# Gates of the attention branch ahead of its products, with the last delta-rule chain between their quarters

## What is computed

```python
proj = h @ w_in + b_in
aq, ak, av, dq, dk_, dv_, dz, db, da, ga, gb = split_cols(proj, IN_SPLITS)
o_att = sliding_window_sink_attention(rope(aq), rope(ak), av, att_sinks)
qkv = silu(causal_depthwise_conv(concat(dq, dk_, dv_), dn_conv_w))
o_dn = gated_rms_norm(gated_delta_rule_chunked(q, k, v, g, beta), dz, dn_norm_g)
y_att = o_att @ w_br_att
y_dn = o_dn @ w_br_dn
merged = sigmoid(ga) * y_att + sigmoid(gb) * y_dn
mix = merged @ w_out
h = layer_norm(ALPHA * h + mix)      # then SwiGLU, a gated input embedding and a second norm
```

## Time and profile before

| | us |
|---|---|
| median of 3 runs | 2249.12 (2247.03 to 2253.12) |
| the profiled execution | 2246.78 |
| its span, first to last instruction | 2245.0 |
| TensorE busy | 2143.2 |
| VectorE busy | 1297.4 |
| ScalarE busy | 1051.5 |
| POOL busy | 70.5 |

### The profile page before, as it was taken

The page is one execution under the profiler, slowest core; times in us unless marked ns, Lnnn a source line. Parts: engine busy times, 40 slices in busy tenths (PEclk is TensorE's granted clock), DMA queues, the critical chain, the costliest instruction groups (busy, mean ns, idle before and its releaser), DMA issues.

```text
span 2245.0 us, 39722 instructions
## 1 busy us (share of the span) xinstructions
PE 2143.2 (95%) x14959; PEld 1986.5 (88%) x14959; DVE 1297.4 (58%) x2182; ACT 1051.5 (47%) x1907; POOL 70.5 (3%) x65
## 2 busy tenths in 40 slices
PE   7999989999899997899999998999999999999997
PEld 6889889889888896799999986899999999998885
DVE  3657665766667655454555557665555555555555
ACT  2446354553554544444544444544444444444442
POOL 1000110100101001000000000000000000000000
PEclk7999999999999999899999999999999999999998
DMA  6564222232232221355555574555555555566552
GB/s 221 187 194 141 90 94 93 76 111 80 88 104 83 93 93 56 103 180 184 177 181 186 172 284 143 188 195 180 179 185 178 187 187 183 176 225 200 189 191 90
DMA packets 279401, 345.13 MB, mean 154 GB/s; under 512 B 6272, under 2 KB 227536, under 8 KB 277936
## 3 DMA queue, kind: packets, MB, share of 16 engines
q1 hardware_dynamic: 277696, 334.78, 46.0%
q0 software_dynamic: 1648, 9.57, 1.1%
HBM read 342.04 MB, written 2.10 MB: 153 GB/s over the span
## 4 chain that ended last, share of the span: by engine, by line
PE 86%; DVE 5%; ACT 5%; issue 3%; DMA 1%; DVEq 0%; ACTq 0%; SPq 0%
PE dense L457 18%; PE dense L458 17%; PE dense L459 17%; PE dense L469 8%; PE dense L470 8%; PE dense L471 8%; PE chain L607 2%; PE chain L604 1%; ACT hi L868 1%; PE chain L595 1%; PE chain L643 1%; PE chain L673 1%; PE chain L626 1%; PE chain L614 1%; PE chain L642 1%
## 5 line engine op out<-in xcount | busy, mean ns | idle before, releaser
L1157 DVE TENSOR_TENSOR lo<-raw,hi 128x512 fp32r<-128x512 f32 x1256 | 846.3, 691 | 615.6 <-ACT hi L868 612.6
L868 ACT ACTIVATE hi<-raw 128x512 fp32r<-128x512 f32 x1256 | 764.7, 629 | 586.6 <-PE dense L459 316.6
L457 PE MATMUL dense<-xh,hi 128*128 128x256 f32 x2944 | 860.5, 292 | 0.0
L459 PE MATMUL dense<-xh,lo 128*128 128x256 f32 x2944 | 835.9, 284 | 0.0
L458 PE MATMUL dense<-xl,hi 128*128 128x256 f32 x2944 | 835.9, 284 | 0.0
L457 PEld LDWEIGHTS dense<-xh,hi 128*128 128x128 f32 x2944 | 567.1, 193 | 21.5 <-issue 13.4
L458 PEld LDWEIGHTS dense<-xl,hi 128*128 128x128 f32 x2944 | 567.7, 193 | 3.6 <-issue 3.6
L459 PEld LDWEIGHTS dense<-xh,lo 128*128 128x128 f32 x2944 | 567.3, 193 | 0.0
L469 PE MATMUL dense<-hi,xh 128*128 128x512 f32 x416 | 163.3, 393 | 4.6 <-issue 3.1
L470 PE MATMUL dense<-hi,xl 128*128 128x512 f32 x416 | 162.9, 391 | 0.0
L471 PE MATMUL dense<-lo,xh 128*128 128x512 f32 x416 | 162.8, 391 | 0.0
(11 more groups left out here) (283 smaller groups left out, 1926.0 us busy)
## 6 DMA issues: line engine op xcount, KB each, us to landing
raw<-in_w_in_dram SPq DMA_DIRECT2D x116, 1024.0 KB, 5.0
raw<-in_w_ffn_gate_dram SPq DMA_DIRECT2D x44, 1024.0 KB, 4.9
raw<-in_w_ffn_up_dram SPq DMA_DIRECT2D x44, 1024.0 KB, 4.9
raw<-in_w_ffn_down_dram SPq DMA_DIRECT2D x44, 1024.0 KB, 5.1
raw<-in_w_br_att_dram SPq DMA_DIRECT2D x16, 1024.0 KB, 5.1
raw<-in_w_br_dn_dram SPq DMA_DIRECT2D x16, 1024.0 KB, 5.3
raw<-in_w_out_dram SPq DMA_DIRECT2D x16, 1024.0 KB, 5.2
raw<-in_w_ple_gate_dram SPq DMA_DIRECT2D x16, 1024.0 KB, 5.1
```

Source lines behind the costliest of these rows:

```text
L457: pe.matmul(o, wh, mh[:, k, :], start=(k == 0), stop=False)
L459: mm = pe.matmul(o, wl, mh[:, k, :], start=False, stop=(k == KT - 1))
L868: act.activation(hi[:, pos.slot(n), :], raw[:, slot, off:off + 512], ACT.Copy).then_inc(sem("hi_ready"), 1)
L1157: dve.tensor_tensor(lo[:, pos.slot(n), :], raw[:, slot, off:off + 512], hi[:, pos.slot(n), :].bitcast(F32), ALU.subtract).then_inc(sem("lo ...
```

## The change

The attention branch no longer goes group by group. All 64 gate quarters come first, right behind the mixer loop, alternating between the two pairs of banks, and each group's tanh is written straight to its place in `merged`. Behind quarter `1 + (c + 1) * 56 // 31` stands stage c of the last chain: stage -1 behind quarter 1, then 0 to 29 behind 2, 4, 6, 8, 10, 11, 13 and so on to 55, 56 quarters for 31 stages. The splits of the attention output stand beside quarters 56 to 63. Then come the 64 quarters of o_att @ w_br_att, also alternating between banks, and one VectorE product per group turns `merged` from tanh to gated product in place. The delta branch is as before.

`merged` moves to a place of its own behind the chain's buffers; the buffers of keys and values for the attention (`kTall`, `vall`), done by then, move to share it. POOL loads `res` as soon as the attention output has been split, and the norm's parameters after the delta branch. SP issues the same units in the new order.

```diff
-TAIL = (0, 4, 6, 9, 12, 17, 20, 23)
+LAST_AT = {1 + (c + 1) * 56 // 31: c for c in range(-1, 30)}
@@ sync
-            for off, w, base in ((GA, A["w_br_att"][0], U_YA), (GB, A["w_br_dn"][0], U_YD)):
-                with sp.Fori(0, 8) as j:
+            for j in range(8):
+                for h in range(2):
+                    load(Pos(4 * U_GA), 2 * j + h, unit_cols(w_in, h, slice(GA + 256 * j, GA + 256 * j + 256)))
...
@@ gpsimd
-            pool.wait_ge(sem("m_lo"), 8)
+            pool.wait_ge(sem("b_lo"), 8)
             pool.dma_start(res[:], A["x"][0].rearrange("(t p) n -> p t n", p=P)).then_inc(sem("res_in"), 16)
+            pool.wait_ge(sem("quarter_done"), 4 * U_OUT)
@@ tensor
-            for k in range(NORMS - LAG, 30):
-                chain_stage(k, PAIRS - 1, False)
-                if k == 0:
+            for n in range(64):
+                j = n // 8
+                if n == 0:
                     pe.wait_ge(sem("pad2"), PAIRS)
-                if k in TAIL:
-                    cols_quarter(Pos(4 * U_YA), TAIL.index(k), TAIL.index(k), 2, xh, xl)
...
+                elif n == 8:
+                    pe.wait_ge(sem("z_in"), PAIRS)
+                elif n % 8 == 0:
+                    pe.wait_ge(sem("gate"), j - 1)
+                cols_quarter(Pos(4 * U_GA), n, n % 8, 2 * ((j + 1) % 2), xh, xl)
+                if n in LAST_AT:
+                    chain_stage(LAST_AT[n], PAIRS - 1, False)
+
+            for n in range(16):
+                if n % 8 == 0:
+                    pe.wait_ge(sem("gate"), 7 + n // 8)
+                if n < 8:
+                    pe.wait_ge(sem("b_lo"), n + 1)
+                cols_quarter(Pos(4 * U_AT), n, n % 8, 2 * ((n // 8 + 1) % 2), bh, bl)
+            with pe.Fori(1, 4) as m:
+                for n in range(16):
+                    if n % 8 == 0:
+                        pe.wait_ge(sem("prod"), 2 * m - 1 + n // 8)
+                    cols_quarter(Pos(4 * U_AT, 16, m), n, n % 8, 2 * ((n // 8 + 1) % 2), bh, bl)
@@ scalar
+            def gate_out(j):
+
+                act.wait_ge(sem("quarter_done"), 4 * U_GA + 8 * j + 8)
+                for f in range(2):
+                    r = act.activation(merged[:, 2 * j + f, :], dense[:, 2 * ((j + 1) % 2) + f, 0:T], ACT.Tanh,
+                                       bias=hbias[:, 2 * j + f:2 * j + f + 1], scale=0.5)
+                r.then_inc(sem("gate"), 1)
+
+            for n in range(64):
+                split(Pos(4 * U_GA + LEAD), n)
+                if n in LAST_AT:
+                    c = LAST_AT[n]
+                    if c == -1:
+                        chain_k(0, PAIRS - 1)
+                        chain_k("norms", PAIRS - 1)
+                    elif c > 0:
+                        chain_k(c, PAIRS - 1)
+                        y_copy(c, PAIRS - 1)
+                if n >= 56:
+                    b = n - 56
+                    if b == 0:
+                        act.wait_ge(sem("on"), 8)
...
+                if n % 8 == 7:
+                    gate_out(n // 8)
@@ vector
+            dve.wait_ge(sem("gate"), 8)
+            with dve.Fori(0, 4) as m:
+                for n in range(16):
+                    split(Pos(4 * U_AT + LEAD, 16, m), n)
+                    if n % 8 == 7:
+                        e = n // 8
+                        dve.wait_ge(sem("quarter_done"), 4 * U_AT + 8 + 8 * e + 16 * m)
+                        g = merged[:, ds(4 * m + 2 * e, 2), :]
+                        b0 = 2 * ((e + 1) % 2)
+                        dve.scalar_tensor_tensor(g, g, 1.0, dense[:, b0:b0 + 2, 0:T], ALU.add,
+                                                 ALU.mult).then_inc(sem("prod"), 1)
```

More of the change, by code:

```diff
@@ L231, in build @@
         vn = place("vn", [P, 2, P])
+        at[0] += -at[0] % 512
+        mg_at = at[0]
+        kTall = place("kTall", [P, PAIRS, 192])
+        vall = place("vall", [P, PAIRS, 2, HD])
         o = [at[0]]
@@ L753, in _, with branch @@
                 mixer_turn(i, True)
-            for k in range(NORMS - LAG, 30):
-                chain_stage(k, PAIRS - 1, False)
-                if k == 0:
+            for n in range(64):
+                j = n // 8
+                if n == 0:
                     pe.wait_ge(sem("pad2"), PAIRS)
-                if k in TAIL:
-                    cols_quarter(Pos(4 * U_YA), TAIL.index(k), TAIL.index(k), 2, xh, xl)
[L762 to L772, removed]
+                elif n == 8:
[16 more added lines that the diff above has]
+                    cols_quarter(Pos(4 * U_AT, 16, m), n, n % 8, 2 * ((n // 8 + 1) % 2), bh, bl)
+            def branch(j, first):
+                pos = Pos(4 * U_YD, 16, j)
+                for k in range(16):
+                    if k == 0:
+                        pe.wait_ge(sem("prod"), 7) if first else pe.wait_ge(sem("gate"), j + 8)
+                    if k == 8:
+                        pe.wait_ge(sem("prod"), j + 8)
+                    if k >= 8:
+                        if first:
+                            pe.wait_ge(sem("b_lo"), 8 + k - 7)
                         cols_quarter(pos, k, k - 8, 0, bh, bl)
@@ L775, in branch @@
                         cols_quarter(pos, k, k, 2, xh, xl)
-            branch(Pos(4 * U_YA, 16, 0), 0, 0, (None, ("z_in", PAIRS)), start=8)
+            branch(0, True)
             with pe.Fori(1, 8) as j:
[L780 to L783, removed]
+                branch(j, False)
             pe.wait_ge(sem("gate"), 16)
@@ L1068, in gates @@
+            with act.Fori(0, 4) as m:
+                for n in range(16):
+                    split(Pos(4 * U_AT + LEAD, 16, m), n)
+            def gates(pos, j, gt_used):
                 for k in range(16):
-                    if k >= start:
-                        split(pos, k)
+                    split(pos, k)
                     if k == 8 - 1:
                         act.wait_ge(sem("quarter_done"), pos.val(8 - LEAD))
-                        if gt_used is not None:
-                            act.wait_ge(sem(gt_used[0]), gt_used[1])
+                        act.wait_ge(sem("prod"), gt_used)
@@ L1484, in _ @@
                 mixer_turn(i, True)
[L1485 to L1507, removed]
+            for n in range(64):
+                split(Pos(4 * U_GA + LEAD), n)
+                if n in LAST_AT:
+                    c = LAST_AT[n]
+                    if c == -1:
+                        chain_k(0, PAIRS - 1)
+                        chain_k("norms", PAIRS - 1)
+                    elif c > 0:
+                        chain_k(c, PAIRS - 1)
+                if n >= 56:
+                    b = n - 56
+                    dve.wait_ge(sem("b_hi"), b + 1)
+                    dve.tensor_tensor(bl[:, 2 * b:2 * b + 2, :].rearrange("p u (t c) -> p u t c", t=TT), att_cols(b),
+                                      bh[:, 2 * b:2 * b + 2, :].rearrange("p u (t c) -> p u t c", t=TT).bitcast(F32),
+                                      ALU.subtract).then_inc(sem("b_lo"), 1)
```

46 lines of the change are left out of this document (19 added, 27 removed).

## The result

The changed kernel took 2215.2 us (median of 4 runs, 2212.7 to 2216.5) beside 2248.1 us for the kernel before (4 runs, 2245.4 to 2253.1). The ratio is 0.985, with a 95% interval of 0.983 to 0.986: 32.8 us faster. Forecast were 2217.5 us, in a range of 2211 to 2228.

A forecast was written before the change was run, and what follows sets the result against it. TensorE's queue was taken to bound the kernel. The region from loop end to delta branch falls from 247.8 to 216.2 us, saving 31.6: 2246.8 - 31.6 = 2215.2 profiled, plus 2.3 gives 2217.5 us, range 2211 to 2228.

The forecast's parts named there:

- What binds: Whole kernel: TensorE, busy for 95% of the span, sets the end with its queue.
- The sum: End of mixer loop to first delta-branch quarter: 184.3 + 31.4 + 0.5 = 216.2 us, against 247.8 before.
- Chain: Last head pair's stages between quarters: 28.2 us priced from the mixer loop plus 3.2 for lengthened quarters, 31.4 us.
- Waits that stay: TensorE in the new tail: only POOL's first inverse level still makes it wait, 0.5 us.
- The key wait: Normed keys in the last chain: the loop's 1.9 us wait goes, with a slack of about 1 us.
- The seam: Between gate quarters and attention products: the 5.7 us wait for split attention rows is hidden by 11.5 us of gate work.
- The clock: New tail: full clock taken for the sum; granted clock 0.98 or more expected, 0.96 kept for the range.
- rival 2: New tail's clock doesn't come back: 4 to 5 us lost at 0.96, 15 at 0.87; chance 0.17 shared with waits.
- Parts costed at nothing: Gate tanh into merged, VectorE's wait and product, SP's order, POOL's earlier x load, ScalarE's tables: 0 us taken.
- The waits only thin out: New tail: late keys, late copies and small scan waits return 7 of 31.6 us, 2223; chance 0.17 shared with clock.
- The queue runs dry: New tail: chain stages hold back ScalarE's and VectorE's splits; slower from 1.2 us a stage; slower given 0.04.
- the signs asked for: Profile after: region about 216 us, no wait over 1 us, clock 0.98 or more, rest of kernel within 2 us.

The follow-up runs named there:

- the late load: Changed kernel with POOL's 2 MB load of x put back to where it was, behind the split of merged: 2214.9 us against 2215.2.
- the three that go on from the change: Changed kernel with attention query rotation moved earlier, 2190.5 us; that plus z's tanh and product behind normed keys and queries, 2196.2; or in the scan, 2191.1.
- the stages packed: Changed kernel with the last chain's 31 stages packed among the first 8 gate quarters, the other 56 following bare: 2242.7 us.
- one stage a quarter: Changed kernel with one stage of the last chain behind each of gate quarters 1 to 31: 2219.9 us.
- the z gate behind the norms: Changed kernel with query rotation moved earlier, plus the tanh of z and its product put behind the normed keys and queries: 2196.2 us.
- the early rotation alone: Changed kernel with the mixer loop's rotation of attention queries moved from quarter 5 to quarter 1: 2190.5 us.

## Why the prediction was right

- *What binds.* TensorE's queue sets the end and nothing behind the region moves: shown by the 1151.6 us behind it, the same in both profiles.
- *The sum.* Region after: forecast 216.2 us, measured 216.5. Dense quarters: 184.3, and 184.32 without the chain. Chain: 31.4 forecast, 32.2 measured with its wait, 31.8 without. Taking stages' prices from the loop's rows, first matmul to next dense matmul plus the lengthened quarter, was good to 0.4 us in sum. The lengthening went in as estimates (0.15 and 0.07 us a stage, 0.4 behind the norms), which no run measured singly, so errors in them may have cancelled.
- *Waits that stay.* The POOL wait of 0.4 us (0.5 forecast) and nothing else. The key wait is gone with 5 quarters and 1.5 us with 3.
- *The seam.* Its 5.7 us wait went, as forecast, but its share is less sharp than I had it: alone it gave 8.0 us in the medians and 2.6 in the region of the one profile.
- *The clock.* Full over the new tail, as the sum had it; the dip or two of rival 2 didn't come, in this profile or in the four others that have this tail (the late load and the three that go on from the change). The Trainium skill ("TensorE: Matmul & The Clock Gate", HAM oscillation) has repeated idle time between groups of matmuls bring the clock down. The new tail has 27 stages between groups of quarters, but TensorE is idle for 0.4 us in all, so this trace has no such idle time to test it with. With the stages packed the trace agrees in kind: TensorE is idle for 3.7 of the 27.5 us from 887.5 us, and the granted clock there is 0.63. (One reading was off: the page's clock line has its dip in the slice from 898 to 954 us and can't show the small ones in the first half, which stand in its nines.)
- *Parts costed at nothing.* The moved load is 0 by its own run. Gate tanh and the new VectorE wait show in no wait of TensorE, and ScalarE loads a table 37 times in both profiles.
- *Rivals.* "The waits only thin out" (1) is what one stage a quarter does: 4.7 us in the medians, 4.1 in the region. (Its price was added up a little high: 2246.8 less 24.6 is 2222.2, not 2223.) "The queue runs dry" (3) decides nowhere in the changed kernel; but I had priced the wrong thing there. I took the lead of six quarters as the reserve that ScalarE and VectorE have. It protects the dense quarters. The chain's own steps stand behind the splits in the same queues and have a margin of only about 1 us in the first stages. In the changed kernel this margin held.
- *The size in time.* 31.6 us forecast, 31.3 in the region, 32.8 in the medians. Not all of the gain in the runs is the region's: 2.7 us of the 34.0 in span lie ahead of it, which the sum had at nothing. So one of the signs asked for, the rest of the same length within 2 us, wasn't met ahead of the region (2.7 us) and was met behind it (0.0). That the median came to within 2.3 us of the forecast owes something to how such executions vary.

What stays open is how the two parts of the old tail's 31 us, 21.9 us of idle time and 9.4 of busy time, hang together. They come together, and no run here holds the clock while TensorE waits.

## What to carry to other kernels

A serial chain costs its owner's work plus its waits; laid between enough independent work on the engine that binds, it costs little more than the work, here 31.8 us and one wait of 0.4, and its price can be read beforehand from a place where it already stands so. Look for such independent work *after* the place where the chain runs out of company, and reorder to bring it forward; one unit of it per stage got most of the gain here (220.6 us of region, against 247.8 and 216.5). Before loading the partner engines further, look for the chain's own steps behind other work in their queues: the reserve that protects the main stream doesn't protect them.

## What the runs showed of the hardware

TensorE's waits and its half clock (1.2 GHz of 2.4) come together, but they don't simply add up. With the waits for queries gone (up to 2.8 us each), 12.4 us less of idle time went with a loop 22.2 us shorter, in which the stretches at half clock fell from nine to three. But nine of these profiles run the same loop, with 7 to 11 such stretches, and those with more of them wait less. The two ends, the loop of the late load with 7 and of one stage a quarter with 11:

```profile
155.96:843.16 687.20, 650.94 (x4904) 597.53 (x4903) 461.24 (x894) 350.22 (x733) 51.44 (x35) 0.98 0.31 96
```
```profile
156.83:845.65 688.82, 656.67 (x4903) 604.00 (x4902) 461.40 (x894) 350.16 (x733) 50.12 (x35) 0.97 0.31 96
```

Four more stretches added 5.7 us of busy time, took 4.1 us of idle time away, and made the loop 1.6 us longer. Where TensorE would have waited anyway, half clock costs it little. Nor does idle time alone bring it: the loop with the z gate behind the norms has 26.7 us of idle time, no listed wait over 1.3 us, and no half clock, against 21.2 us and three stretches with the early rotation alone.

ScalarE loads a table on the way from logarithm (L981) to exponential (L983) in each turn, 1.28 us, with the next activation 0.01 us behind it. In the changed kernel:

```profile
851.32 0.68 ACT L981 ACTIVATE qh<-chain,epsc 128x512 f32<-128x512 f32 x1
852.02 1.28 ACT L983 ACT_TABLE_LOAD   x1
853.31 0.63 ACT L983 ACTIVATE kh<-kh 128x512 f32<-128x512 f32 x1
```

The Trainium skill ("ScalarE: Activation LUTs", What ACT_TABLE_LOAD costs) has about 2.66 us for a switch, of which about 1.28 are the load and the rest a drain. These traces agree on the load and show no drain: about 1.3 us from the end of one activation to the start of the next. The Trainium skill ("ScalarE: Activation LUTs", Table sets: the hidden batching unit) also has one set that holds both functions, with one load for both. In these traces a load stands between them every time.
